# A ring of seven gathered row pairs in place of eight

## The reference, cut to what matters

```python
def peer_block(xb, w_query, sub_keys, u_tab, v_tab):      # xb: 128 tokens x 1024
    q = (xb @ w_query).reshape(T, PEER_HEADS, 2, PEER_DK // 2)
    s = jnp.einsum('thcd,hcnd->thcn', q, sub_keys).astype(jnp.float32)
    s1, i1 = lax.top_k(s[:, :, 0], PEER_TOPK)
    s2, i2 = lax.top_k(s[:, :, 1], PEER_TOPK)
    ...
    top_s, pos = lax.top_k(cand_s, PEER_TOPK)
    e = jnp.take_along_axis(cand_i, pos, axis=-1)         # (T, 8, 16) expert numbers
    gate = jax.nn.softmax(top_s, axis=-1)
    act = jax.nn.gelu(jnp.einsum('thkd,td->thk', u_tab[e], xb).astype(jnp.float32))
    return jnp.einsum('thk,thkd->td', (gate * act).astype(xb.dtype), v_tab[e])
```

## Time and profile before

| | us |
|---|---|
| median of 3 timed runs | 4033.66 (4028.71 to 4036.87) |
| time of the profiled execution | 4021.95 |
| its span, first to last instruction | 4020.1 |
| PE busy | 2858.3 (71%) |
| DVE busy | 2654.0 (66%) |
| ACT busy | 1485.8 (37%) |
| POOL busy | 1368.1 (34%) |
| gathers (line 1270) | 1056 |
| moved over the span | 1248.22 MB, mean 310 GB/s |

### The profile page before, as it was taken

One profiled execution on the slowest core, in us unless ns is written; L12 is line 12 of the kernel. 1 busy time (PEld: TensorE's weight loads), 2 busy tenths in 40 slices (PEclk: granted clock), 3 DMA queues, 4 the chain that ended last, 5 costly groups with the idle time before them and its releaser, 6 DMA issues.

```text
span 4020.1 us, 53279 instructions
## 1 busy us (share of the span) xinstructions
PE 2858.3 (71%) x18798; PEld 1340.5 (33%) x18798; DVE 2654.0 (66%) x6645; ACT 1485.8 (37%) x3026; POOL 1368.1 (34%) x1230
## 2 busy tenths in 40 slices
PE   6999777736666676667767676777777766767656
PEld 3545566615222232223223232332323322232211
DVE  1376233342877777877877787678768776777776
ACT  1121222113426234532743483267338522332222
POOL 0000000000443544454354435334444545453421
PEclk8999999868888778878878887888789887788778
DMA  2101100015999999999999999999999999999964
GB/s 81 40 27 59 59 1 0 2 63 181 411 417 408 417 412 411 411 413 415 404 406 414 410 385 417 417 405 404 417 411 405 390 418 413 412 416 411 406 261 169
DMA packets 225745, 1248.22 MB, mean 310 GB/s; under 512 B 33200, under 2 KB 62032, under 8 KB 90224
## 3 DMA queue, kind: packets, MB, share of 16 engines
q0 software_dynamic: 160256, 1132.54, 69.1%
q1 hardware_dynamic: 65264, 112.87, 7.9%
HBM read 1232.20 MB, written 13.11 MB: 310 GB/s over the span
## 4 chain that ended last, share of the span: by engine, by line
DMA 34%; DVE 15%; PE 13%; ACT 7%; issue 5%; POOL 4%; SPq 0%; DVEq 0%; ACTq 0%; POOLq 0%
DMA uv_rows<-in_peer_uv,expert 28%; PE peer_y L1896 8%; DVE uv_rows L1535 5%; DMA pages_ring<-out_k_new 5%; POOL uv_rows L1270 3%; PE peer_s L1713 2%; ACT L1686 1%; ACT diag L1694 1%; ACT L1632 1%; PE peer_y L1892 1%; DVE same L1316 1%; DVE same L1314 1%; DVE pick L1318 1%; DVE weights L1342 1%; PE beside L1734 1%
## 5 line engine op out<-in xcount | busy, mean ns | idle before, releaser
L1896 PE MATMUL peer_y<-uv_rows,diag 64*64 64x512 f32 x8192 | 1285.7, 758 | 793.6 <-ACT diag L1694 772.7
L1270 POOL DMA_INDIRECT uv_rows<-in_peer_uv,expert x1056 | 1201.3, 1138 | 1712.4 <-PE peer_y L1896 1316.2
L1535 DVE CUSTOM_DVE_ANT_0 uv_rows<-uv_rows,p_h 128x1024 f32<-128x1024 f32 x1056 | 1276.5, 1225 | 512.7 <-DMA uv_rows<-in_peer_uv,expert 508.7
L1896 PEld LDWEIGHTS peer_y<-uv_rows,diag 64*64 64x64 f32 x8192 | 318.8, 160 | 1489.0 <-ACT diag L1694 1106.9
L1694 ACT ACTIVATE diag<-p_ident,weights 128x128 f32<-128x128 f32 x1024 | 355.2, 394 | 498.7 <-DVE weights L1342 496.3
L1686 ACT ACTIVATE gelu<-hidden 128x2 f32<-128x2 f32 x528 | 107.4, 203 | 1120.2 <-DVE hidden L1535 1116.1
L523 PE MATMUL proj<-mix,w_in_tile 128*128 128x512 f32 x672 | 298.0, 602 | 18.3 <-DVE mix L332 18.3
L1713 PE MATMUL peer_s<-wk,p_h2t 128*128 128x256 f32 x1152 | 280.1, 398 | 2.3 <-ACT p_h2t L1585 1.3
L1713 PEld LDWEIGHTS peer_s<-wk,p_h2t 128*128 128x128 f32 x1152 | 222.2, 198 | 107.6 <-issue 76.7
L1686 ACT ACT_TABLE_LOAD x196 | 251.5, 1283 | 3.5
L633 POOL COPY v_c<-prc 128x192 f32 (+1 forms) x17 | 5.8, 343 | 627.4 <-POOLq L86 347.5
(11 more groups left out here) (324 smaller groups left out, 3935.6 us busy)
## 6 DMA issues: line engine op xcount, KB each, us to landing
w_out_rows<-in_w_out SPq DMA_DIRECT2D x72, 512.0 KB, 8.1
uv_rows<-in_peer_uv,expert POOLq DMA_INDIRECT x1056, 12.5
w_in_tile<-in_w_in SPq DMA_DIRECT2D x24, 512.0 KB, 3.8
uv_rows<-in_w_query SPq DMA_DIRECT2D x4, 2048.0 KB, 10.1
pages_ring<-out_k_new SPq DMA_DIRECT2D x36, 192.0 KB, 31.7
pages_ring<-out_v_new SPq DMA_DIRECT2D x36, 192.0 KB, 25.8
p_x<-in_x_rows SPq DMA_DIRECT2D x9, 512.0 KB, 8.0
mix<-in_xT SPq DMA_DIRECT2D x8, 528.0 KB, 6.8
```

Source lines behind the costliest of these rows:

```text
L1270: pool.indirect_dma_start(out=uv[:, m % RING, :], out_offset=None, in_=io["peer_uv"], in_offset=bass.IndirectOffsetOnAxis(ap=expert[:, t % ...
L1535: nc.vector.tensor_tensor_reduce(out=uv[:, m % RING, 0:D], in0=uv[:, m % RING, 0:D], in1=h2[:, b % 2, :], scale=1.0, scalar=0.0, op0=ALU.m ...
L1896: ins = nc.tensor.matmul(Y[r][rows[j], :], diag[rows[r], m % (2 * GP), rows[r]], uv[rows[r], m % RING, D + j * 512:D + (j + 1) * 512], sta ...
```

## The change

The ring has seven slots in place of eight. `uv_rows` becomes 56 KB in each partition in place of 64 KB; nothing else takes the 8 KB. There is one semaphore `uv_in` fewer. Each place that says `m % RING` and the wait `m - RING + 1` of GpSimd follow.

```diff
@@ -969,7 +969,7 @@
 def peer(nc, io, sb):

-    RING = 8
+    RING = 7
     GP = 2
     PAGES = 8
     HN = 2 * KEYS
```

## The result

The ring of seven is slower: 4056.16 us in the median of five timed runs (4047.09 to 4068.15) against 4036.87 for the kernel before (4028.71 to 4040.49). The ratio is 1.0057, 95% interval 1.0033 to 1.0082, or 23 us (13 to 33). The forecast was 4050 in a range of 4030 to 4080, from an addition of 16.7 us.

A forecast was written before the change was run, and what follows sets the result against it. The 16 DMA engines were taken as the bound during the prompt gathers. Only the dips counted, 16.7 us, the other terms being taken as 0; added to the timed median 4033.66 this gave 4050, range 4030 to 4080.

The forecast's parts named there:

- the loop's own part: Steady state: of a slot's round, 9.7 us outside the transfer stay; 4.0 us remain above the floor, cost 0 to 0.5 us.
- the signs: Profile after: landing median near 9.8 us, VectorE's wait for landings up by about the time lost, share 1.01, GB/s 0.6% lower.
- The start of the gathers: First gathers: the eighth is issued at about 1010.94 us; cost 0 to 1 us, taken as 0.
- wait of TensorE for a cache page: Cache page fetches queued behind a waiting gather start 2.8 us later; hidden, cost 0, or 20 us without cover.
- Term 2: Dips in the prompt gathers: DMA engines run dry one turn of 2.78 us in six stretches, 16.7 us; bounds 7.0 and 30.4.
- rival C: Not slower, even faster: SyncE's transfers get through sooner and close the dips, gain at most 4.4 us, 4029; chance 0.05.
- Rival A: No difference that can be told, under 0.2% or 8 us; dips cost 4 to 7 us, 4039; chance 0.28.
- Rival B: Holes count everywhere: all 22 stretches of the prompt gathers lose one turn, 61 us, 4095; chance 0.11.
- Term 5: Run-out from 3830 us: a turn's fourth gather waits for the first pick of the turn between; 0 to 2 us, taken as 0.
- held-up issues: Some gather issues on GpSimd are held up about 1.06 us; 6 us at the six dips, left to the range.

The follow-up runs named there:

- depth seven and eight slots: Against the kernel before: eight slots stay in memory, only GpSimd waits for the release of gather m - 7 in place of m - 8; ratio 1.0061.
- seven slots and Copy: Seven slots, with Copy in place of Exp, Ln and Exp on ScalarE in the prompt attention; ratio 1.0010 to the kernel before.
- the earlier loads: SyncE loads the late attention's queries and first K and V tiles before waiting for the next block's h2; ratio 1.0015 with eight slots, 1.0070 with seven.

## Why the prediction was right, and where its size was off

The direction and the mechanism came out as put. The landing median fell by about one turn, 12.5 to 10.1 us (9.8 expected); the loop's own part stayed within a microsecond (seven turns of 2.80 us less the landing median: 9.5 us, and 10.4 with depth seven and eight slots, against 9.7); six slots showed the reserve running out; the depth alone reproduced the whole effect. VectorE's wait for landings grew by 24.2 us for 26.0 lost, as the signs said; the rate fell by 1%, not by 0.6 (406 GB/s, 408 forecast). The start of the gathers showed no cost (the first turn of block 0 is 0.5 us shorter after), and no wait of TensorE for a cache page has appeared. That the timed median came within 6 us of the forecast is in part luck: the interval is 13 to 33 us, the terms that were off all lie on one side, and the stages grew by 26.0 and 2 to 4 us.

Term 2 was mis-sized: 16.7 us forecast, 26.0 measured. It counted one turn in each of the six stretches whose shortest landing was under 8.6 us. The losses aren't confined to these. From the first dot product of a block to that of the next (the last one to its last), in us:

| block | 0 | 1 | 2 | 3 | 4 | 5 | 6 | 7 |
|---|---|---|---|---|---|---|---|---|
| before | 341.5 | 355.8 | 357.8 | 360.3 | 361.8 | 362.9 | 356.7 | 342.7 |
| after | 347.5 | 359.5 | 364.4 | 363.8 | 364.6 | 364.0 | 359.1 | 342.4 |
| six slots | 372.0 | 378.5 | 372.5 | 385.8 | 378.5 | 382.7 | 374.6 | 372.4 |

Blocks 1 and 4 had none of the six stretches and lost 3.7 and 2.8 us. Block 7, beside which no prompt attention runs, lost nothing with seven slots (with six it lost 30 us); block 6, where the attention ends with the fifth pair, still lost 2.4. What one block loses isn't fixed to better than 3 us: with depth seven and eight slots block 2 lost 3.6 us and block 5 2.9. The marks of 40 us with their least landing were too coarse an instrument: what decides is a hole in the issues against the reserve at that moment. The upper end of the term, 30.4 us, which had reckoned with such holes, was the nearer one; the price of a single dip also has a part that I hadn't seen, the slower packets.

The length of a pause alone doesn't say which hole costs, either. The longest pause between two gathers of the kernel before is 11.9 us, and the DMA share stays at 1.02 through it:

```profile
1212.91 0.94 POOL L1270 DMA_INDIRECT uv_rows<-in_peer_uv,expert  x1 [0.30 <-issue]
1224.77 1.64 POOL L1270 DMA_INDIRECT uv_rows<-in_peer_uv,expert  x1 [10.93 <-PE peer_y L1896]
1215.00:1225.00 10.00, 4.45 (x20) 2.02 (x24) 7.90 (x19) 6.09 (x12) 0.23 (x1) 0.66 1.02 410
```

With seven slots the pause at this place is 10.7 us and the share there 1.03. Just before it four gathers had gone out within 4.5 us; before the hole of 7.0 us that made a dip the last four had taken 6.7 us, so what was queued had had more time to drain. That is part of the difference only, and what the rest is wasn't tried. And pauses over 7 us between two gathers are as many with seven slots and Copy as with seven alone, 46.

The dips of the kernel before were read wrongly. I took them as the ring of eight falling short, the start of a loss. Those at 2380 and 3160 are there with nine slots too, and the deepest, 0.82 at 2400, isn't in a second execution of the same kernel. So the case for rival C (they could be closed) had no ground. C had also held that the waits for SyncE's transfers are on the path: with seven slots TensorE's wait for K tiles fell from 80.6 to 67.3 us and the kernel became slower, and with the earlier loads it went from the stretch altogether, and the stretch with eight slots grew. Rival A had the dips' lower end, 7 us; it is excluded by the interval (13 to 33 us). Rival B, all 22 stretches, 61 us, is too. It was right that the loss isn't confined to the six stretches; whether it falls on its 22 wasn't compared, and at 2.78 us each they were too dear.

Term 5 was taken as 0 with an upper end of 2. Measured, the run-out grew by 3.7 us in the profiled pair and by 2.5 between the means of the two groups, and the gather that I named makes about one of them at most, in the one execution that tests it.

The rules of the Trainium skill left the sum alone, and that was right. The shortest landing after is 5.4 us, between the 5.8 of the earlier trace rows and what the fit of "DMA: Bandwidth & Descriptors" ("Anatomy of one DMA") gives with the issue on top, an estimate of 0.94 + 4.4 = 5.3 us. Nor do the held-up issues of the prediction decide: GpSimd was busy for 1333.7 us of the stretch in the profile after and for 1308.8 us in the run with depth seven and eight slots, and the stretches are 2865.2 and 2864.8 us.

```profile
1018.00:3883.00 2865.00, 1981.46 (x11266) 804.08 (x11266) 2133.97 (x5506) 1233.10 (x2488) 1308.82 (x1148) 0.83 1.01 406
```

## What to carry to other kernels

Where the DMA engines are the bound, a ring's depth is reserve against the holes in the issues, not against the mean. The time from issue to landing shows it: its median less its minimum is the reserve (6.7 us with eight slots here), one slot is one turn of it (2.8 us), and the stretches where it nears the minimum are those in danger. This tells the direction and the order of size; the loss itself came out 1.6 times the estimate. The curve is flat, then steep (nine to eight slots 1 us, eight to seven 26, seven to six 152), so try one step on either side before giving the memory away. If the 8 KB are needed, look at the pauses first: without the attention's table loads on ScalarE, the slot was worth 8.5 us and not 26. And when an edit is meant to remove a loss, compare it with its own control stage by stage: the earlier K loads removed one step and made another, and the total alone showed nothing.

## What was not expected of the hardware

The DMA share stayed at 1.01 while the rate fell from 410 to 406 GB/s over the stretch: packets of 8 KB were on the mean 319.6 ns long with eight gathers in flight, 321.4 with seven and 329.4 with six, at an unchanged median of 313 ns with eight and seven. The long ones stand where the queue has run low. In the ring of seven, packets that start in the three microseconds behind one with a share under 0.8 take 363.6 ns on the mean (362.5 in the kernel before, 373.2 with six slots), and those away from such places 319.6. So the share understates what a thin queue costs, and the rate is the number to read.
